# Half-size raw weight pieces, feed-forward up pieces three chunks ahead, their product on VectorE, layer loops unrolled

## What is computed

```python
def squared_relu_mlp(h, w_up, w_down):
    u = jax.nn.relu(h @ w_up)
    return (u * u) @ w_down

def conv_ffn(h, w_up, conv_w, conv_b, w_down):
    S = h.shape[1]
    u = h @ w_up
    up = jnp.pad(u, ((0, 0), (CONV_WIDTH - 1, 0), (0, 0)))
    u = conv_b + up[:, 0:S] * conv_w[0]
    for j in range(1, CONV_WIDTH):
        u = u + up[:, j:j + S] * conv_w[j]
    gate, val = jnp.split(u, 2, axis=-1)
    return (jax.nn.silu(gate) * val) @ w_down
```

## Time and profile before

| | |
|---|---|
| runs of the kernel before | 1503.28 us median (1503.16, 1503.28, 1508.17) |
| the profiled execution | 1507.45 us, span 1505.6 us |
| mean granted TensorE clock | 0.966 |
| PE matmul busy | 1394.4 us (93%), 8766 matmuls |
| DVE busy | 873.3 us (58%) |
| ACT busy | 736.8 us (49%) |
| POOL busy | 243.4 us (16%) |
| transfers | 231.1 MB, mean 153 GB/s |

### The profile page before, as it was taken

The page is one execution under the profiler, slowest core; times in us unless marked ns, Lnnn a source line. Parts: engine busy times, 40 slices in busy tenths (PEclk is TensorE's granted clock), DMA queues, the critical chain, the costliest instruction groups (busy, mean ns, idle before and its releaser), DMA issues.

```text
span 1505.6 us, 22092 instructions
## 1 busy us (share of the span) xinstructions
PE 1394.4 (93%) x8766; PEld 1239.4 (82%) x8766; DVE 873.3 (58%) x1028; ACT 736.8 (49%) x948; POOL 243.4 (16%) x220
## 2 busy tenths in 40 slices
PE   6977999999999899999997899999689888999995
PEld 6955889989987689899896789999578666899994
DVE  4542655556645456554569566666647764666664
ACT  4376544445344345444458355545453445545543
POOL 0012000000400000000004113333204133033332
PEclk9999999999999999999999899999898889999998
DMA  7630555554654246555363145555443101445541
GB/s 255 222 113 0 189 200 178 195 194 142 216 175 168 84 155 213 183 191 195 135 215 112 57 169 172 189 171 172 163 168 112 57 29 56 141 168 183 181 168 56
DMA packets 32616, 231.10 MB, mean 153 GB/s; under 512 B 3616, under 2 KB 3616, under 8 KB 5408
## 3 DMA queue, kind: packets, MB, share of 16 engines
q1 hardware_dynamic: 31104, 224.41, 43.7%
q10 hardware_dynamic: 1440, 5.68, 1.0%
HBM read 229.03 MB, written 1.05 MB: 153 GB/s over the span
## 4 chain that ended last, share of the span: by engine, by line
PE 60%; ACT 11%; DVE 11%; issue 7%; POOL 6%; DMA 3%; ACTq 0%; DVEq 0%; POOLq 0%; SPq 0%
PE ps L545 18%; PE ps L546 18%; PE ps L547 18%; POOL arena L460 5%; ACT w_hi L1037 4%; DVE w_lo L1405 3%; DMA ring<-ws 2%; ACT arena L1119 2%; DVE arena L1544 1%; DVE arena L1549 1%; PE ps L523 1%; ACT arena L1124 1%; PE ps L962 1%; DVE arena L1462 1%; POOL arena L494 1%
## 5 line engine op out<-in xcount | busy, mean ns | idle before, releaser
L1405 DVE TENSOR_TENSOR w_lo<-ring,w_hi 128x2048 fp32r<-128x2048 f32 x212 | 486.7, 2297 | 362.8 <-ACT w_hi L1037 362.7
L1037 ACT ACTIVATE w_hi<-ring 128x2048 fp32r<-128x2048 f32 x212 | 405.0, 1912 | 291.8 <-PE ps L547 179.5
L545 PE MATMUL ps<-x_hi,w_hi 128*128 128x256 f32 x1664 | 472.7, 284 | 8.4 <-DVE w_lo L1405 5.8
L546 PE MATMUL ps<-x_lo,w_hi 128*128 128x256 f32 x1664 | 471.8, 284 | 0.0
L547 PE MATMUL ps<-x_hi,w_lo 128*128 128x256 f32 x1664 | 471.7, 283 | 0.0
L545 PEld LDWEIGHTS ps<-x_hi,w_hi 128*128 128x128 f32 x1664 | 320.2, 192 | 10.8 <-DVE w_lo L1405 6.2
L546 PEld LDWEIGHTS ps<-x_lo,w_hi 128*128 128x128 f32 x1664 | 320.2, 192 | 1.2
L547 PEld LDWEIGHTS ps<-x_hi,w_lo 128*128 128x128 f32 x1664 | 320.2, 192 | 0.0
L545 PE MATMUL ps<-w_hi,y_hi 128*128 128x512 f32 (+1 forms) x624 | 248.1, 398 | 30.0 <-POOL y_lo L464 19.6
L546 PE MATMUL ps<-w_lo,y_hi 128*128 128x512 f32 (+1 forms) x624 | 244.3, 392 | 0.0
L547 PE MATMUL ps<-w_hi,y_lo 128*128 128x512 f32 (+1 forms) x624 | 243.6, 390 | 0.0
(11 more groups left out here) (211 smaller groups left out, 1346.4 us busy)
## 6 DMA issues: line engine op xcount, KB each, us to landing
ring<-ws SPq DMA_DIRECT2D x212, 1024.0 KB, 4.9
tab<-tables ACTq DMA_DIRECT2D x4, 550.0 KB, 5.3
rowg<-rows ACTq DMA_DIRECT2D x3, 512.0 KB, 6.2
h<-x SPq DMA_DIRECT2D x2, 512.0 KB, 5.9
out<-arena SPq DMA_DIRECT2D x2, 512.0 KB, 2.6
arena<-decay ACTq DMA_DIRECT2D x1, 768.0 KB, 6.8
sm<-small ACTq DMA_DIRECT2D x1, 746.0 KB, 5.8
arena<-narrow ACTq DMA_DIRECT2D x1, 296.0 KB, 4.7
```

Source lines behind the costliest of these rows:

```text
L545: mm(o, lh, rh, start=start, stop=False, skip_group_check=True)
L546: mm(o, lh, rl, start=False, stop=False, skip_group_check=True)
L1037: A(w_hi[:, s, :], ring[:, g % RAW, :], ACT.Copy).then_inc(hi_ready, 1)
L1405: V.tensor_tensor(w_lo[:, s, :], ring[:, g % RAW, :], w_hi[:, s, :].bitcast(F32), ALU.subtract)\
```

## The change

- The raw slots are four of half a piece (128 x 1,024). `stream`, `hi` and `lo` work in halves q = 2g and 2g + 1: two transfers of 512 KB, two ACT copies, two DVE subtractions per piece. `w_hi` and `w_lo` keep their four whole slots, and PE waits for both halves.
- The order of a feed-forward part is given by `ahead`. It is 1 for the MLP, as it was, and 3 for the FFN. The FFN keeps four chunks of `y` tiles and closes with the last two down pieces together (`closing` = 2); the weights are laid out in the new order.
- In the FFN the product and `y_lo` move from POOL to DVE, one unit late: on DVE the order in unit u is `scaled(u)`, `product(u-1)`, `w_lo` of the refill, `y_lo(u-1)`, the taps of u. On ACT it is base(u), `y_hi(u-1)`, `w_hi` of the refill, silu(u). POOL has no part in it.
- The register loops of MLP and FFN are unrolled on all engines; the one on SP stays, over halves.
- The first constants (gains, identity) come in a transfer of their own; the rest of `sm` is loaded later on ACT's queue. PE runs ten small matmuls on `ones` before it waits for the first transfer.
- In NSA, ACT's refills for the key and value pieces stand ahead of the copies `ns_raw` of the same unit; the norm after the first FFN has two late refills in place of one.

The core of the diff:

```diff
-RAW = 2
+HALF = PIECE // 2
+RAW = 4
...
-        mlp_h = [Hidden(g, MLP_C, 2, 3) for g in G_MLP]
-        ffn_h = [Hidden(g, FFN_C, 1, 2) for g in G_FFN]
+            def run(self, up, down):
+                for c in range(self.chunks + self.ahead):
+                    if c < self.chunks:
+                        up(c)
+                    if c >= self.ahead:
+                        down(c - self.ahead)
+
+        mlp_h = [Hidden(g, MLP_C, 2, 1, 2, 1) for g in G_MLP]
+        ffn_h = [Hidden(g, FFN_C, 1, 3, 4, 2) for g in G_FFN]
...
+                if turn is not None or q >= RAW:
+                    sp.wait_ge(lo_ready, plus(q - RAW + 1, turn, RAW))
+                g, c = q // 2, (q % 2) * HALF
+                src = ws[g][:, c:c + HALF] if turn is None else \
+                    ws[bass.ds(turn * (RAW // 2) + g, 1), :, c:c + HALF].rearrange("a p n -> p (a n)")
+                sp.dma_start(ring[:, q % RAW, :], src).then_inc(weights_in[q % RAW], 16)
...
+            pe.wait_ge(ones_ready, 1)
+            for _ in range(10):
+                mm(ps[:, 3, 0:P], ones[:, :], ones[:, :], start=True, stop=True, skip_group_check=True)
             pe.wait_ge(loaded, 16)
...
-            act.dma_start(sm[:, :], small).then_inc(loaded, 16)
+            act.dma_start(sm[:, 0:S_CONV], small[:, 0:S_CONV]).then_inc(loaded, 16)
...
+            def hi(g):
+                for q in (2 * g, 2 * g + 1):
+                    c = (q % 2) * HALF
+                    act.wait_ge(weights_in[q % RAW], 16 * (q // RAW + 1))
+                    A(w_hi[:, g % RING, c:c + HALF], ring[:, q % RAW, :], ACT.Copy).then_inc(hi_ready, 1)
...
+                        for e in range(2):
+                            r = A(conv[:, u % 2, e, :], conv_in[:, u % 2, e, :], ACT.Identity,
+                                  scale=par(u, 4 + e), bias=par(u, 6 + e))
+                        r.then_inc(base, 1)
+                        if u:
+                            product_hi(u - 1)
+                        refill(st.up(c) + u % 2)
+                        act.wait_ge(conv_done, u + 1)
+                        A(silu[:, u % 2, :], conv[:, u % 2, 0, :], ACT.Silu).then_inc(sl, 1)
...
+            def lo(g):
+                for q in (2 * g, 2 * g + 1):
+                    v = slice((q % 2) * HALF, (q % 2 + 1) * HALF)
+                    dve.wait_ge(hi_ready, q + 1)
+                    V.tensor_tensor(w_lo[:, g % RING, v], ring[:, q % RAW, :], w_hi[:, g % RING, v].bitcast(F32),
+                                    ALU.subtract).then_inc(lo_ready, 1)
...
+                        dve.wait_ge(done, g + 1)
                         scaled(conv_in[:, u % 2, :, :], ps[:, bank(u), :], scale).then_inc(freed, 1)
+                        if u:
+                            product(u - 1)
+                        refill(g)
+                        if u:
+                            product_lo(u - 1)
+                        dve.wait_ge(freed, u + 1)
+                        dve.wait_ge(base, u + 1)
```

More of the change, by code:

```diff
@@ L450, in _ @@
             norm_power(6)
[L452 to L469, removed]
             norm_power(7)
@@ L588, in add, with accumulate @@
                 return r
-            def accumulate(g, tiles, first, turn=None, each=0):
-                split(g, turn, each)
+            def accumulate(g, tiles, first):
+                split(g)
                 for k in range(2):
@@ L635, in down @@
                         for i, (g, tiles) in enumerate(pieces):
-                            accumulate(g, tiles, c == 0 and i == 0, turn, st.each)
-                st.run(pe, up, down)
+                            accumulate(g, tiles, c == 0 and i == 0)
+                st.run(up, down)
             def transpose_pair(b, src, g):
@@ L1031, in sumsq, with refill @@
                     A(xs[:, t, :], h[:, t, :], ACT.Square, accum_out=ssq[:, t:t + 1]).then_inc(ss_ready, 1)
[L1033 to L1039, removed]
+            def hi(g):
[3 more added lines that the diff above has]
+                    A(w_hi[:, g % RING, c:c + HALF], ring[:, q % RAW, :], ACT.Copy).then_inc(hi_ready, 1)
+            def refill(g):
                 if g + RING < G_END:
-                    act.wait_ge(done, plus(g + 1, turn, each))
-                    hi(g + RING, turn, each)
+                    act.wait_ge(done, g + 1)
+                    hi(g + RING)
             def gain(n, k):
@@ L1126, in up, with down @@
-                        A(y_hi[:, 4 * (c % 2) + u % 2, :], prod[:, u % 2, :], ACT.Copy).then_inc(hh, 1)
-                def down(c, turn):
-                    if c < st.chunks - 1:
-                        for i in range(st.dn):
-                            refill(st.down(c) + i, turn, st.each)
-                st.run(act, up, down)
+                    if u == units - 1:
+                        product_hi(u)
+                def down(c):
+                    if c < st.chunks - st.closing:
+                        refill(st.down(c))
@@ L1536, in up, with product_lo @@
+                def product_lo(u):
+                    dve.wait_ge(pr, u + 1)
+                    dve.wait_ge(hh, u + 1)
+                    i = st.tiles(u // 2)[u % 2]
+                    V.tensor_tensor(y_lo[:, i, :], prod[:, u % 2, :], y_hi[:, i, :].bitcast(F32), ALU.subtract)\
+                     .then_inc(ready, 1)
+                def up(c):
                     for u in (2 * c, 2 * c + 1):
                         g = st.up(c) + u % 2
-                        dve.wait_ge(done, plus(g + 1, turn, st.each))
+                        dve.wait_ge(done, g + 1)
@@ L1547, in up @@
                         for e in range(2):
                             v = conv[:, u % 2, e, 2:T]
[L1549 removed]
+                            r = V.scalar_tensor_tensor(v, conv_in[:, u % 2, e, 0:T - 2], par(u, e), v,
                                                        ALU.mult, ALU.add)
                         r.then_inc(conv_done, 1)
[L1552 to L1557 removed]
@@ L1559, in ffn, with down @@
-                if n == 0:
-                    dve.wait_ge(scale_ready, SCALE_OF[6] + 1)
-                else:
-                    dve.wait_ge(scale_ready, SCALE_OF[8] + 1)
-                st.run(dve, up, down)
+                    if u == units - 1:
+                        product(u)
+                        product_lo(u)
+                def down(c):
+                    if c < st.chunks - st.closing:
+                        refill(st.down(c))
+                dve.wait_ge(scale_ready, SCALE_OF[6 if n == 0 else 8] + 1)
```

236 lines of the change are left out of this document (102 added, 134 removed).

## The result

The changed kernel takes **1517.82 us** (median of 4 runs, 1516.6 to 1520.56), the kernel before beside it 1503.34 (1503.16 to 1508.17): ratio 1.0091, with a 95% interval of 1.0066 to 1.0116. It is slower, by 14.5 us in the medians.

A forecast was written before the change was run, and what follows sets the result against it. The FFN's vector-engine loop, 18.7 us a chunk against PE's 17.0, was taken to bound the changed kernel. FFN +26.9, halves -2.1, GLA -3, NSA -7, start -2: +12.8 us on the median, 1516.1 us; range 1494 to 1531.

The forecast's parts named there:

- The unit: FFN vector loop, from one `scaled` to the next: 7.47 us a unit after the change.
- steps 1 to 5: FFN loop from `scaled(u)` through ACT's base, `y_hi`, half `w_hi`, then DVE's `w_lo`, `y_lo` and taps: 7.47 us.
- The down refill: FFN unit that also refills a down piece: 11.27 us, 3.80 us more than a plain unit.
- The new wait: FFN, DVE: `w_lo` waits for ACT's first half of `w_hi`, holding up everything behind it, some 2 us a unit.
- Closing: End of each FFN: two down pieces instead of one come after the last tile, +5.45 us each.
- Start: Kernel start: the first transfer falls from 746 KB to 106 KB, -2 us (between 0 and -4).
- The ten matmuls: Kernel start on PE: they end before `x` is there, 0 us.
- The first two mixers: Half pieces shorten the chain from raw piece to whole `w_lo` by 0.7 us, once in each mixer.
- GLA: ACT's 3.09 us transfer wait among the decays shrinks by 2.3, plus 0.7 from halves: -3 us (0 to -5).
- The half transfer: Ring transfer of half a piece takes 3.7 us, between 2.45 and 4.9.
- NSA: Key and value pieces: refills ahead of copies and early raw pieces cut PE's waits, -7 us (between -2 and -10).
- Unrolling: MLP and FFN loops: no change; the MLP is PE's, the FFN's 7.47 us is already straight-line work.

The follow-up runs named there:

- experiment 2: The changed kernel with ACT's `w_hi` of the refill ahead of `y_hi(u-1)` in the FFN; 1505.41 us.
- experiment 1: The changed kernel with DVE's `y_lo(u-1)` and refill `w_lo` moved behind the taps in the FFN; 1466.54 us, ratio 0.9741 to the kernel before.
- experiment 3: The changed kernel with the FFN's product and `y_lo` on POOL again, in the order of the kernel before, `w_lo` behind the taps; 1466.27 us.
- experiment 5: The kernel before with MLP and FFN loops unrolled and raw pieces in halves, old order, one chunk ahead, old start; 1473.36 us.
- experiment 6: The changed kernel with one closing down piece per FFN (`closing` = 1) and one late refill in the following norm; 1513.67 us.
- experiment 8: The changed kernel with `w_lo` behind the taps, but `sm` in one first transfer and without the ten matmuls; 1467.81 us.
- experiment 9: The changed kernel with `w_lo` behind the taps and only the ten small matmuls left out; 1466.25 us.
- experiment 4: The kernel before with only the register loops of MLP and FFN unrolled; 1494.67 us.
- experiment 10: The changed kernel with `w_lo` behind the taps, and ACT's NSA key and value refills behind the `ns_raw` copies again; 1467.76 us.

## Why the prediction was right, and where its sizes were off

The forecast was 1516.1 us, the kernel took 1517.82: the side, the mechanism and the time stand. That the time is so close is partly luck. The sum was worked out against one execution and then added to the median; on the profiled pair it is 3.2 us too high (+12.8 against +9.6), and on the medians 1.7 too low. And the stretches of the table miss by up to 2.8 us each, in both directions.

**The unit** (steps 1 to 5): 7.47 forecast, 7.42 measured, and 7.11 with `y_hi` out of the way (experiment 2). The down refill: 11.27 forecast, 11.21 measured. First to last `scaled` 181.7 for 182.8 us. The new wait is the 2.09 us in front of `w_lo`, and it takes from PE what was said: in the first FFN seven waits for `w_lo` of 1.01 to 1.06 us, ahead of the second to the eighth down piece (the first ends at 944.2 us), and 10.9 us ahead of `close`. Experiment 1 shows the cause: with only that order changed the loss is gone. Experiment 3 shows that the product's engine isn't it, experiment 5 that the halves by themselves aren't.

**Closing**: 5.45 us in each FFN forecast. Experiment 6 shows 5.5 in the second. In the first, from `close` to the first transpose of the next norm, it is 6.53 us before and 9.97 after, +3.4; dropping the second piece wins nothing there, as DVE's refills come between (11.0 us in experiment 6).

**Start**: -2, and -0.7 for the halves there. The first matmul of piece 0 starts at 16.15 us before and 13.73 after, -2.4. With halves and the old start (experiments 5 and 8) it starts at 15.33 and 15.43. So both sizes are about right on this chain: 0.7 to 0.8 for the halves, 1.6 to 1.7 for the new start. In the whole time experiment 8 finds 1.3 us for the new start. The ten matmuls were put at 0; they hold the transposes back by 0.4 us and bring the end of piece 0 forward by 1.3 (experiment 9), and the medians show neither. (The first `scaled` of the kernel moved by 4.9 us, from 32.16 to 27.28, but that compares two single executions: experiment 4, with the start of before, has it at 29.46.)

**The first two mixers**: -1.4 forecast. The residual of the first mixer, DVE's first `h<-ps,h`, starts at 158.07 us before and 154.35 after. That is -3.7, for -3.4 forecast up to there with the start. The second mixer, from one norm's first transpose to the next, takes 209.7 and 209.35 us, -0.3 for -0.7. At the first `scaled` of FFN 1 halves with the old start (experiments 5 and 8) are 3 to 4 us ahead of whole pieces (887.74 and 888.47 for 891.76 and 892.18), and the new start gives about 1 more (886.0 to 887.4 in seven executions).

**GLA** is the term that failed: -3 forecast, nothing found. From the first transpose ahead of GLA to the first ahead of FFN 1 it is 140.0 us before and 140.1 after, and 138.6 and 138.8 in experiments 4 and 5, again the same with whole pieces and with halves. ACT's wait for the transfer among the decays did shrink, from 3.09 us to 0.72 and 0.55. The step that failed is the overlap: it was taken for granted that what ACT wins there reaches PE. In the chain that ended last of the changed kernel no transfer stands in this place any more, but DVE from 793.47 to 821.50 us: its halves of `w_lo` and its own subtractions and multiplications. Here the last of them, on that chain:

```profile
813.55 5.56 DVE arena L1718 x4
819.12 2.39 DVE arena L1718 x2
```

PE's wait behind them is 9.16 us, for 8.48 before. The half transfer, put at 3.7 us, has a median of 4.8, but this is no flat price: the 82 halves issued while no other was in flight have 3.8, near the forecast, and the 255 issued while one was have 4.8. The Trainium skill (DMA: Bandwidth & Descriptors, Anatomy of one DMA) gives an estimate of 3.2 us for a half, by a fit made on the GpSimd path; the ring's transfers are SyncE's, and the shortest of the 424 took 3.55 us. With no term for GLA the sum would have been +15.8.

**NSA**: -7 forecast, -7.4 found: from its first transpose to that of the next norm it is 207.7 us before (1083.86 to 1291.52) and 200.3 after (1088.41 to 1288.70). With the +3.4 of closing and -0.4 behind it this makes the -4.4 of the table. The waits went from 8.30 to 3.06 us on PE's timeline:

```profile
1128.55 1.09 PE L493 MATMUL ps<-sm,h 128*128 128x128 f32 x8 [0.78 <-DVE arena L1444]
...
1131.92 2.15 PE L493 MATMUL ps<-sm,h 128*128 128x128 f32 x8 [2.28 <-DVE x_lo L1403]
```

That is 5.2 us of the 7.4. The mean PEclk of the stretch rose with it, from 0.91 to 0.95; the trace doesn't separate what share of that reached the time. The size was right, but the prediction gave most of it to the order of ACT's refills. The halves alone, in the old order, take this stretch from 206.9 us (experiment 4) to 198.6 (experiment 5), and experiment 10 leaves 2 us to the order.

**Unrolling** was put at 0, since "the 7.47 is already straight-line work". For the kernel after that holds, but the rows of before came from straight-line units at the end (20 and 21), while the register loop in the middle ran at 17.7 us a chunk. The loss in the FFN was therefore measured against a kernel with that handicap: it entered through the earlier trace rows and did no harm to the sum. It hid, however, that an unrolled kernel in the old order would win 10 us.

**What the change would have brought.** Unrolled 1494.67, and halves 1473.36, and three ahead with the new start and NSA 1466.3 (experiments 1 and 3). Two steps put too early on DVE turn 39 us of gain (the ratio of experiment 1) into 14 of loss. The versions of experiments 1 and 3 beat both kernels and are equal.

## What to carry to other kernels

When work moves to an engine that runs its list in order, write down for each item when its input is made, and put what waits longest at the end of the round; here the taps, which the other engine needs, stood behind a copy that it made last. Price a new order by the sum round the loop and not by busy shares: DVE, busy for 70% of the window (114.5 of 163 us), lay on the loop that set the pace. Before a shorter wait is booked as a gain, follow the other engines to the same place, as DVE in GLA. Price a smaller piece in every loop that goes through it, and test the parts of a mixed change alone, as the good ones may be hidden by one bad one.

## What the runs showed of the hardware

- POOL's product of 128 x 256 takes 2.3 us beside a `w_lo` of 128 x 2,048, 1.20 beside halves, 0.72 alone. It cuts both ways: two `w_lo` halves of DVE take 2.35 us, and 2.90 with the product beside them, as in DVE's timelines of experiments 1 and 3. This one is of experiment 3:

```profile
982.17 2.90 DVE L1400 TENSOR_TENSOR w_lo<-ring,w_hi 128x1024 fp32r<-128x1024 f32 x2
...
982.79 1.20 POOL L447 TENSOR_TENSOR arena<-arena 128x256 f32<-128x256 f32 x1 [3.56 <-ACT arena L1119]
```

- The product ends some 0.6 us after the end of the `w_lo` that it met: at 1069.89 for 1069.30 in the earlier trace rows, and at 983.99 above, where a half of 1.22 us ends at 983.39. That is near its 0.72 alone, as if it had been held until then. That agrees with the Trainium skill (SBUF — State Buffer, Who interferes with whom): a DVE operation with two inputs in SBUF and a POOL operation that reads SBUF take turns at a shared port. So a shorter `w_lo` shortened POOL's wait here. In GLA it is DVE that pays: its multiplications of 128 x 512 take 0.68 us alone and 1.75 to 1.78 beside one of POOL, in both kernels.
- What a transfer of 512 KB took went with what else of the ring was in flight. These two of the changed kernel were issued at 329.16 us, with none other of the ring in flight, and at 330.27, behind the first:

```profile
ring<-ws SPq DMA_DIRECT2D x1, 512.0 KB, 3.7
ring<-ws SPq DMA_DIRECT2D x1, 512.0 KB, 5.1
```

- The medians are 3.8 us with none in flight at the issue, 4.8 with one, 5.3 with two, and 4.8 over all. One of 1 MB took 4.9, with none or one in flight.
- The register loop cost 0.5 us per chunk of the FFN against the same code unrolled (experiment 4), where the vector engines' loop set the pace.
- With ten small matmuls ahead of the first real ones the granted clock fell to half and rose again earlier: piece 0 ran at 0.12 us a matmul from 16.94 us on, for 19.69 without them. The medians show no gain from it (experiment 9).
